# Prompt attention in blocks of 256 queries, two heads abreast, with fp32r scores and V as the stationary operand

## The chip, the cores and the metric

The kernel runs on one NeuronCore of a Trainium2 chip. The metric is the device time of one launch in microseconds. The time of before is the median of three runs. A profile is one further execution, recorded by the hardware profiler; times in its rows are microseconds from the start of the recorded span. PE is TensorE (PEld its weight loads), DVE is VectorE, ACT is ScalarE, POOL is GpSimd, SP is SyncE, which here only issues DMAs.

## What is computed

A two-layer decoder trunk of width 1024 serves one prompt of 1024 tokens and 8 sample requests of 4 new tokens each. Layer 0 mixes tokens with a causal convolution module, layer 1 with forgetting attention (16 heads of 64), and each is followed by a SwiGLU FFN. The change lies in the prompt part of layer 1's attention:

```python
c = jnp.cumsum(logf, axis=1)
s = jnp.einsum('bqhd,bkhd->bhqk', qi, k, preferred_element_type=jnp.float32) * scale
s = s + ci[:, :, :, None] - cT[:, :, None, :]
s = jnp.where(kpos[None, :] <= qpos[:, None], s, -jnp.inf)
pr = jax.nn.softmax(s, axis=-1)
return jnp.einsum('bhqk,bkhd->bqhd', pr.astype(v.dtype), v)
```

The term of the query's own c is the same for a whole row and falls out of the softmax; the kernel adds only the key's.

## The kernel before

All of the kernel is one launch with an instruction stream for each engine, ordered by semaphores. Most of its time goes to dense products: weights and activations are each split into a high and a low fp32r part, and three products hi*hi, lo*hi and hi*lo are summed in PSUM (`unit_block`, L673 to L675), over three blocks of 352 tokens. A "unit" is one 128-column slice of a weight, a pair of units is one step `q`. For each unit SP loads `wraw`, ACT writes `whi` (L1127), POOL writes `wlo` (L606), and PE waits for `w_lo`.

Three stages of layer 1 concern us, in this order.

1. Projection (24 units: 8 of q, 8 of k, 8 of v). DVE copies each unit from PSUM into `stg`, and ACT issues one DMA to a scratch tensor in HBM, `q_scr` or `k_scr` (`store_staged`), since attention needs heads on partitions 0 to 63. Keys and values are also transposed on PE for the outputs; the values stay in `Vt`, tokens on partitions. `negc`, the negative sum of the log forget gates, goes to `c_scr` through `negct`.

2. Prompt attention. It loops over 8 pairs of heads (`prompt_pair`), and in each over 16 tiles `t` of 128 queries: first the 8 of one head, then those of the other, in the order `ORDER = [3, 2, 1, 0, 7, 6, 5, 4]` of the query tile `qt`, each with its `(qt + 1) * 128` keys. For a tile PE makes the scores in fp32 from `qa` (64 rows of q and a row of ones) and `ka` (64 rows of k and the row of c) into two PSUM banks (L963); DVE adds the causal mask to the diagonal block (L1766) and takes the negative maximum (L1768); ACT takes exp with the sum as by-product (L1404) into `pr`, two buffers; PE transposes `pr` in blocks of 128 (L921), one tile late; ACT copies these to `pt` (L1391); PE multiplies, with `pt` as the stationary side and 64 columns of V moving (L937), two tiles late; DVE divides by the sum (L1745, L1751) into `on`; four such are transposed (L948) and copied to `OT` (L1756). SP loads a head's `qa` and `ka` when the tiles of the head before it have been scored (`load_head`). POOL has nothing to do.

3. Cache attention for the 8 requests. SP loads 64 pages of keys (`kr`) and 64 of values (`vr`), 512 KB each, four buffers of each; the first four key pages are issued while prompt attention still runs. PE transposes keys (L995), makes scores on four groups of 32 output partitions (L1011), and multiplies with the values likewise (L1050). The `cb_scr` scratch carries the sums of the cached gates (`cbT`), stored by ACT at the start of stage 2 (L1382).

The order of work within each engine is the order of the program; there are no priorities.

Of the kernel before, what the change touches and what calls it, by code (L numbers as in the profile page):

```python
# [28 lines left out]
F32 = mybir.dt.float32  # L29
# [7 lines left out]
P = 128  # L37
# [3 lines left out]
def hybrid_step(nc, x_prompt, x_sample, state_conv, cache_k, cache_v, cache_logf, page_table,  # L41
# [37 lines left out]
    with ExitStack() as ctx:  # L79
# [93 lines left out]
        negct = at("negct", [H, SEQ], F32, after("negc"))  # L173
        NM = at("NM", [NS, NREQ, H, TNEW], F32, after("negct"))
# [13 lines left out]
        qa = at("qa", [DH + 1, 2, SEQ], F32, where["xhi"][0])  # L188
        ka = at("ka", [DH + 1, 2, SEQ], F32, after("qa"))
        pr = at("pr", [P, 2, SEQ], F32, after("ka"))  # L190
        pt = at("pt", [P, 2, SEQ], F32, after("pr"))
        on = at("on", [P, NT, P], F32, where["tm"][0])
# [16 lines left out]
        ob = at("ob", [P, 2, P], F32, where["negct"][0])  # L209
# [4 lines left out]
        q_scr = nc.dram_tensor("q_scr", (D, SEQ), F32).ap()  # L214
        k_scr = nc.dram_tensor("k_scr", (D, SEQ), F32).ap()
        c_scr = nc.dram_tensor("c_scr", (H, SEQ), F32).ap()
# [58 lines left out]
        nqk = sem("nqk")  # L275
        stg_st = [sem("stg_st0"), sem("stg_st1")]
# [14 lines left out]
        a_ld = [sem("a_ld0"), sem("a_ld1")]  # L291
        a_sc = sem("a_sc")
        a_mk = sem("a_mk")
        a_max = sem("a_max")
        a_exp = sem("a_exp")
        a_tr = sem("a_tr")
        a_pt = sem("a_pt")
        a_pv = sem("a_pv")
        a_rec = sem("a_rec")
        a_on = sem("a_on")  # L300
        o_tr = sem("o_tr")
# [65 lines left out]
        NTILES = C * NTAU  # L367

        ORDER = [3, 2, 1, 0, 7, 6, 5, 4]
# [23 lines left out]
        def _(sp):  # L393
# [87 lines left out]
            load_pairs(Q_ATTN_OUT, 1, attn_w_out[0], 0, C, two)  # L481

            for s in range(2):
                sp.wait_ge(mm[s], Q_ATTN_OUT * NB)
            for s in range(2):
                sp.wait_ge(stg_st[s], 16 * C)
            sp.wait_ge(c_st, 16)

            def load_head(i, s):
                h = i * 2 + s  # L490
                sp.dma_start(qa[0:DH, s, :], q_scr[ds(h * DH, DH), :]).then_inc(a_ld[s], 16)
                sp.dma_start(ka[0:DH, s, :], k_scr[ds(h * DH, DH), :]).then_inc(a_ld[s], 16)
                sp.dma_start(ka[DH:DH + 1, s, :], c_scr[ds(h, 1), :]).then_inc(a_ld[s], 16)
            load_head(0, 0)
            load_head(0, 1)
            with sp.Fori(1, C) as i:
                for s in range(2):

                    sp.wait_ge(a_sc, i * NTAU + (NT * (s + 1) - NTAU))
                    load_head(i, s)  # L500
# [27 lines left out]
            for s in range(2):  # L528
                sp.wait_ge(kt_st[s], 16 * C // 2)
            for n in range(4):  # L530
                load_k(n)

            sp.wait_ge(a_pv, NTILES)
            sp.wait_ge(w_lo, 2 * Q_ATTN_OUT + 2)
# [7 lines left out]
            for n in range(NP):  # L542
                load_v(n)
                if n + NPG + 4 < NP:
                    load_k(n + NPG + 4)
                if n % NPG == 1 and n // NPG + 1 < NREQ:
                    load_sums(n // NPG + 1)
# [18 lines left out]
        def _(pool):  # L566
# [71 lines left out]
            with pool.Fori(Q_ATTN_IN + 1, QK) as q:  # L638
                low_parts(q)


            with pool.Fori(QK, Q_ATTN_OUT + 1) as q:
                low_parts(q)
# [3 lines left out]
            pool.wait_ge(a_pv, NTILES)  # L647
            nc.gpsimd.memset(cbx[:, :, :], 0.0).then_inc(d_z, 1)
            nc.gpsimd.memset(PTs[:, :, :, :], 0.0).then_inc(d_z, 1)
            nc.gpsimd.memset(PTn[:, :, :], 0.0).then_inc(d_z, 1)  # L650
            with pool.Fori(Q_ATTN_OUT + 1, Q_FFN1 + 1) as q:
                low_parts(q)
# [6 lines left out]
        def _(pe):  # L659
# [221 lines left out]
            pe.wait_ge(c_nc, 2)  # L881
# [32 lines left out]
            pe.wait_ge(a_ones, 1)  # L914

            def probs_tr(base, t):

                pe.wait_ge(a_exp, base + (t + 1))
                past(pe, a_pt, base + t)
                for kb in range(ORDER[t % NT] + 1):  # L920
                    m = nc.tensor.transpose(PS[:, 4 + kb // 4, (kb % 4) * P:(kb % 4 + 1) * P],  # L921
                                            pr[:, t % 2, kb * P:(kb + 1) * P], ident[:, :])
                m.then_inc(a_tr, 1)

            def values(i, base, t):

                pe.wait_ge(a_pt, base + (t + 1))
                past(pe, a_on, base + (t - 1))

                if t == NTAU - 1:  # L930
                    pe.wait_ge(o_ev, i * 2 + 1)
                elif t == 1:
                    past(pe, o_ev, i * 2)
                nb = ORDER[t % NT] + 1
                for kb in range(nb):
                    v = Vt[:, kb, ds(i * P + (t // NT) * DH, DH)]
                    m = nc.tensor.matmul(PS[:, 6 + t % 2, 0:DH],  # L937
                                         pt[:, t % 2, kb * P:(kb + 1) * P], v,
                                         start=(kb == 0), stop=(kb == nb - 1))
                m.then_inc(a_pv, 1)  # L940

            def outputs_tr(i, half):

                pe.wait_ge(a_on, i * NTAU + (NTAU - 2 + 2 * half))
                if half == 1:
                    pe.wait_ge(o_ev, i * 2 + 1)
                for j in range(4):
                    m = nc.tensor.transpose(PS[:, 7, j * P:(j + 1) * P], on[:, 4 * half + j, :], ident[:, :])  # L948
                m.then_inc(o_tr, 1)

            def prompt_pair(i):
                base = i * NTAU
                first = isinstance(i, int)
                for t in range(NTAU):
                    s, qt = t // NT, ORDER[t % NT]
                    if t % NT == 0:
                        pe.wait_ge(a_ld[s], i * 48 + 48)

                    past(pe, a_exp, base + (t - 1))
                    nk = (qt + 1) * P  # L960
                    for k0 in range(0, nk, 512):
                        k1 = min(nk, k0 + 512)
                        m = nc.tensor.matmul(PS[:, 2 * (t % 2) + k0 // 512, 0:k1 - k0],  # L963
                                             qa[:, s, qt * P:(qt + 1) * P], ka[:, s, k0:k1],
                                             start=True, stop=True)
                    m.then_inc(a_sc, 1)
                    if t >= 1:
                        probs_tr(base, t - 1)
                    elif not first:
                        probs_tr(base - NTAU, NTAU - 1)  # L970
                    if t >= 2:
                        values(i, base, t - 2)
                    elif not first:
                        values(i - 1, base - NTAU, NTAU + t - 2)
                    if not first and t in (0, 2):
                        outputs_tr(i - 1, t // 2)

            prompt_pair(0)
            with pe.Fori(1, C) as i:
                prompt_pair(i)  # L980
            probs_tr((C - 1) * NTAU, NTAU - 1)
            values(C - 1, (C - 1) * NTAU, NTAU - 2)
            outputs_tr(C - 1, 0)
# [937 lines left out]
```

## Time and profile before

| | us |
|---|---|
| median of 3 runs (lowest, highest) | 3260.32 (3250.59, 3261.3) |
| the profiled execution, its time | 3277.89 |
| its span | 3276.1 |
| mean granted clock of TensorE in it | 0.934 |
| projection of layer 1, from 1331 to 1637 | 306 |
| prompt attention, from 1652 to 2075 | 423 |
| cache attention, from 2077 to 2340 | 263 |

The span goes from the first to the last instruction; the execution's own time has 1.8 us around it. The granted clock is 1.00 at 2.4 GHz and 0.50 at 1.2 GHz.

### The profile page before, as it was taken

How to read it: one execution, taken by the hardware profiler on the slowest of the kernel's cores; microseconds unless marked ns; L12 is line 12 of the kernel's file. 1: busy time of each engine (PE TensorE's matmuls, PEld its weight loads, DVE VectorE, ACT ScalarE, POOL GpSimd, SP SyncE). 2: the span in 40 equal slices, each digit the busy share in tenths (PEclk: the TensorE clock that was granted, in tenths of full speed). 3: DMA queues.
4: the chain of work that ended last, by engine and by line, in shares of the span. 5: the costliest groups of instructions: out<-in, count | busy, mean ns of one | idle time of the engine just before them, and what ended most of it. 6: DMA issues, size and time to landing. Idle time of an engine off the chain costs nothing.

```text
span 3276.1 us, 49541 instructions
## 1 busy us (share of the span) xinstructions
PE 2939.1 (90%) x18658; PEld 2725.1 (83%) x18658; DVE 1095.4 (33%) x1876; ACT 924.1 (28%) x1533; POOL 782.6 (24%) x378
## 2 busy tenths in 40 slices
PE   5786698999999999999999999777799999999997
PEld 4786497999999998899977777555688999999997
DVE  5899634111111114411135445433332111111114
ACT  4555533211111113211124334322223212111123
POOL 2899423222221213311200000000022222222221
PEclk8888799999999999999969779978899999999998
DMA  3101011111111111234102001477411111111111
GB/s 93 39 26 33 19 45 33 40 50 45 36 49 37 53 40 50 73 86 113 42 24 74 20 19 45 167 253 275 151 39 39 37 53 39 44 45 37 53 35 69
DMA packets 243435, 206.63 MB, mean 63 GB/s; under 512 B 18188, under 2 KB 218892, under 8 KB 243076
## 3 DMA queue, kind: packets, MB, share of 16 engines
q1 hardware_dynamic: 230215, 186.66, 18.5%
q10 hardware_dynamic: 13133, 18.80, 1.7%
q8 instruction: 55, 0.90, 0.1%
q14 instruction: 32, 0.26, 0.0%
HBM read 183.16 MB, written 23.13 MB: 63 GB/s over the span
## 4 chain that ended last, share of the span: by engine, by line
PE 51%; issue 32%; POOL 8%; DVE 6%; ACT 2%; DMA 1%; DVEq 0%; ACTq 0%; SPq 0%; POOLq 0%
PE PS L673 17%; PE PS L675 16%; PE PS L674 16%; POOL yp L629 7%; DVE tm L1511 2%; POOL wlo L606 1%; DVE rs L1490 1%; DMA xin<-in_x_prompt 1%; DVE hlo L1553 1%; PE PS L800 0%; DVE xlo L1496 0%; ACT prods L1240 0%; ACT tm L1282 0%; ACT xhi L1138 0%; DVE yn L1884 0%
## 5 line engine op out<-in xcount | busy, mean ns | idle before, releaser
L673 PE MATMUL PS<-xhi,whi 128*128 128x352 f32 x3456 | 1144.8, 331 | 134.0 <-DVE u L1605 54.2
L675 PE MATMUL PS<-xlo,whi 128*128 128x352 f32 x3456 | 1121.7, 325 | 0.0
L674 PE MATMUL PS<-xhi,wlo 128*128 128x352 f32 x3456 | 1121.4, 324 | 0.0
L606 POOL TENSOR_TENSOR wlo<-wraw,whi 128x1024 fp32r<-128x1024 f32 x208 | 497.9, 2395 | 1867.0 <-ACT whi L1127 1867.0
L673 PEld LDWEIGHTS PS<-xhi,whi 128*128 128x128 f32 x3456 | 657.9, 190 | 177.8 <-DVE u L1605 56.1
L674 PEld LDWEIGHTS PS<-xhi,wlo 128*128 128x128 f32 x3456 | 661.0, 191 | 0.0
L675 PEld LDWEIGHTS PS<-xlo,whi 128*128 128x128 f32 x3456 | 658.9, 191 | 0.0
L1127 ACT ACTIVATE whi<-wraw 128x1024 fp32r<-128x1024 f32 x208 | 218.9, 1052 | 593.1 <-PE PS L675 565.1
L1548 DVE TENSOR_TENSOR ht<-PS,ht 128x352 f32<-128x352 f32 x132 | 69.1, 524 | 906.7 <-PE PS L675 902.7
L673 PE MATMUL PS<-hhi,whi 128*128 128x352 f32 x1056 | 341.2, 323 | 8.8 <-issue 8.8
L674 PE MATMUL PS<-hhi,wlo 128*128 128x352 f32 x1056 | 338.5, 321 | 0.0
L675 PE MATMUL PS<-hlo,whi 128*128 128x352 f32 x1056 | 338.2, 320 | 0.0
L1534 DVE TENSOR_TENSOR X<-PS,X 128x352 f32 x216 | 113.2, 525 | 447.3 <-PE PS L675 447.0
L673 PEld LDWEIGHTS PS<-hhi,whi 128*128 128x128 f32 x1056 | 198.1, 188 | 10.8 <-issue 10.8
L674 PEld LDWEIGHTS PS<-hhi,wlo 128*128 128x128 f32 x1056 | 198.4, 188 | 0.0
L675 PEld LDWEIGHTS PS<-hlo,whi 128*128 128x128 f32 x1056 | 197.9, 187 | 0.0
L629 POOL TENSOR_TENSOR yp<-yp,prods 128x1024 f32<-128x1024 f32 x80 | 191.1, 2388 | 11.8 <-POOL yp L629 0.4
L1628 DVE SCALAR_TENSOR_TENSOR PS<-u,par,PS 128x1024 f32<-128x1024 f32 x144 | 185.7, 1289 | 4.8
L963 PE MATMUL PS<-ka,qa 65*128 65x512 f32 (+3 forms) x384 | 182.8, 592 | 3.1 <-issue 3.1
L1182 ACT ACTIVATE hhi<-ht 128x352 f32 x132 | 65.5, 498 | 410.4 <-DVE ht L1548 410.4
L937 PEld LDWEIGHTS PS<-Vt,pt 128*128 128x128 f32 x1152 | 164.1, 221 | 11.9 <-issue 7.0
L937 PE MATMUL PS<-Vt,pt 128*128 (+1 forms) x1152 | 167.9, 299 | 3.6 <-DVE OT L1756 3.6
(184 smaller groups left out, 2386.9 us busy)
## 6 DMA issues: line engine op xcount, KB each, us to landing
wraw<-in_ffn_w_gu SPq DMA_DIRECT2D x88, 512.0 KB, 3.7
kr<-in_cache_k SPq DMA_DIRECT2D x64, 512.0 KB, 6.5
vr<-in_cache_v SPq DMA_DIRECT2D x64, 512.0 KB, 8.1
wraw<-in_ffn_w_down SPq DMA_DIRECT2D x32, 384.0 KB, 3.0
wraw<-in_attn_w_in SPq DMA_DIRECT2D x24, 512.0 KB, 3.8
wraw<-in_ffn_w_down SPq DMA_DIRECT2D x32, 320.0 KB, 2.8
wraw<-in_conv_w_in SPq DMA_DIRECT2D x16, 512.0 KB, 3.9
wraw<-in_conv_w_out SPq DMA_DIRECT2D x8, 512.0 KB, 3.5
```

The costliest lines, as they stand in the source:

```text
L606: nc.gpsimd.tensor_tensor(wlo[:, s, :], wraw[:, s, :], whi[:, s, :].bitcast(F32), ALU.subtract).then_inc(w_lo, 1)
L629: nc.gpsimd.tensor_tensor(yp[:, :], prods[:, 0, :] if i == 1 else yp[:, :], prods[:, i % 3, :], ALU.add).then_inc(p_tap, 1)
L673: nc.tensor.matmul(out, wh, hi[:, k, blk(b)], start=(k == 0), stop=False)
L674: nc.tensor.matmul(out, wl, hi[:, k, blk(b)], start=False, stop=False)
L675: m = nc.tensor.matmul(out, wh, lo[:, k, blk(b)], start=False, stop=(k == kc - 1))
L937: m = nc.tensor.matmul(PS[:, 6 + t % 2, 0:DH], pt[:, t % 2, kb * P:(kb + 1) * P], v, start=(kb == 0), stop=(kb == nb - 1))
L963: m = nc.tensor.matmul(PS[:, 2 * (t % 2) + k0 // 512, 0:k1 - k0], qa[:, s, qt * P:(qt + 1) * P], ka[:, s, k0:k1], start=True, stop=True)
L1127: nc.scalar.activation(whi[:, s, :], wraw[:, s, :], ACT.Copy).then_inc(w_hi, 1)
L1511: return nc.vector.scalar_tensor_tensor(tm[:, tmi(b, c), :], X[:, c, blk(b)], par[:, c, row:row + 1], rs[:, b, :], ALU.mult, ALU.mult)
L1534: nc.vector.tensor_tensor(xs, PS[:, NB * s + b, 0:BW], xs, ALU.add).then_inc(ev[s], 1)
L1548: nc.vector.tensor_tensor(ht[:, b, :], PS[:, NB + b, 0:BW], ht[:, b, :], ALU.mult).then_inc(ev[1], 1)
L1628: nc.vector.scalar_tensor_tensor(yacc, u[:, k:k + SEQ], w[:, R_DW + k:R_DW + k + 1], yacc, ALU.mult, ALU.add).then_inc(cv, 1)
```

## The change

Prompt attention is written anew, fully unrolled, and its inputs are prepared otherwise.

- Tiles: pairs of heads as before, but the tiles alternate between the heads, `qt` from 7 down to 0. Two query tiles of both heads make a block of 256 queries, 4 blocks in a pair, 32 in all.
- Scores: fp32r. While staging, ACT makes `sth`, the high part, POOL makes `stl`, the low part, and ACT issues three stores for each unit of q and two for each of k. `qa` is [hi; hi] on 128 rows, `kau` and `kal` are [lo; hi], `qb` is [lo; 1; 1] and `kbu`, `kbl` are [hi; c high; c low] on 66. The mask is added by PE, as a product of `identr` and `cmaskr`.
- The lower 512 keys are double buffered, the upper ones are loaded in two parts as they come free.
- P is divided by its sum before the transposes, on POOL, in place, with four buffers of `pr`. The transposes come three tiles late.
- Of the transposes' two PSUM banks ACT copies one and DVE the other, into `pta` or `ptb`, where the two query tiles of a block lie side by side; below `qt` 4 each tile uses one bank.
- Values: V is the stationary side (64 columns), 256 columns of P transposed move, head 0 writes output partitions 0 to 63 and head 1 64 to 127, in three portions that come between scores and transposes. The result lies as `OT` needs it, and DVE copies it.
- Buffers: `pr` lies over `stg` and `kr`, `ptb` over `cbT`, `sth` and `stl` over `Vt`. So exp waits for the stores of `cbT` and of the keys, max for those of `cbT`, and all key pages are loaded after attention. The first pair of weights of the output projection is loaded and split during stage 3.

```diff
-        ORDER = [3, 2, 1, 0, 7, 6, 5, 4]
+        def tile(g):
+            i, t = g // NTAU, g % NTAU
+            return i, t % 2, NT - 1 - t // 2
+        def portions(n):
+            kts = list(range(2 * block_of(n)[1] + 2))
+            a, e = (len(kts) + 1) // 3, (2 * len(kts) + 1) // 3
+            return [kts[0:a], kts[a:e], kts[e:]]
...
# SP
+            load_upper(0, SEQ - QW)
+            load_keys(0)
+            load_upper(0, HALF)
+            load_lower(0)
+            load_keys(1)
+            for i in range(1, C):
+                sp.wait_ge(a_sc, NTAU * (i - 1) + 4)
+                load_upper(i, SEQ - QW)
+                sp.wait_ge(a_sc, NTAU * (i - 1) + 8)
+                load_upper(i, HALF)
+                sp.wait_ge(a_sc, NTAU * i)
+                load_lower(i)
+                if i + 1 < C:
+                    load_keys(i + 1)
...
# POOL
+            def staged_lows(q):
+                for s in range(2):
+                    pool.wait_ge(w_hi, q * 2 + (s + 3))
+                    nc.gpsimd.tensor_tensor(wlo[:, s, :], wraw[:, s, :], whi[:, s, :].bitcast(F32),
+                                            ALU.subtract).then_inc(w_lo, 1)
+                    pool.wait_ge(qk_hi, q * 2 + (s + 1 - 2 * Q_ATTN_IN))
+                    nc.gpsimd.tensor_tensor(stl[:, s, :], stg[:, s, 0:SEQ], sth[:, s, :].bitcast(F32),
+                                            ALU.subtract).then_inc(qk_lo, 1)
...
+            for g in range(TILES):
+                i, h, qt = tile(g)
+                pool.wait_ge(a_rec, g + 1)
+                probs = pr[:, g % 4, 0:(qt + 1) * P]
+                nc.gpsimd.tensor_scalar(probs, probs, rden[:, g % NTAU:g % NTAU + 1], None, ALU.mult).then_inc(a_nrm, 1)
...
# PE
+            def prompt_scores(g):
...
+                past(pe, a_exp, g - 1)
...
+                for k0 in range(0, nk, HALF):
+                    n = min(nk - k0, HALF)
+                    out = PS[:, 2 * (g % 2) + k0 // HALF, 0:n]
+                    k1, k2 = (kau[:, h, 0:n], kbu[:, h, 0:n]) if k0 else (kal[:, i % 2, h, 0:n], kbl[:, i % 2, h, 0:n])
+                    last = k0 + n == nk
+                    nc.tensor.matmul(out, q1, k1, start=True, stop=False)
+                    nc.tensor.matmul(out, q2, k2, start=False, stop=not last)
+                m = nc.tensor.matmul(PS[:, 2 * (g % 2) + qt // 4, (qt % 4) * P:(qt % 4 + 1) * P], identr[:, :],
+                                     cmaskr[:, :], start=False, stop=True)
+                m.then_inc(a_sc, 1)
...
+            def prompt_values(n, part):
...
+                for kt in portions(n)[part]:
+                    c0 = P if kt == 2 * bn + 1 else 0
+                    for h in range(2):
+                        m = nc.tensor.matmul(PS[DH * h:DH * h + DH, 6 + n % 2, c0:QW],
+                                             Vt[:, kt, (2 * i + h) * DH:(2 * i + h + 1) * DH],
+                                             block_probs(n)[:, h, kt, c0:QW], start=(kt == 0),
+                                             stop=(kt == 2 * bn + 1), skip_group_check=True)
...
+            for g in range(TILES + 6):
+                if g < TILES:
+                    prompt_scores(g)
+                if g >= 7:
+                    n, part = divmod(g - 7, 4)
+                    if part < 3:
+                        prompt_values(n, part)
+                if 3 <= g < TILES + 3:
+                    probs_tr(g - 3)
...
# ACT
+            act.wait_ge(cb_st, 16 * NREQ)
...
+            for g in range(TILES + 3):
+                if g >= 3 and uses(g - 3)[0]:
+                    probs_out(g - 3)
+                if g < TILES:
+                    prompt_exp(g)
...
# DVE
+            dve.wait_ge(cb_st, 16 * NREQ)
+            for g in range(TILES + 6):
+                if g < TILES:
+                    prompt_max(g)
+                if 1 <= g <= TILES:
+                    prompt_rec(g - 1)
+                if 3 <= g < TILES + 3 and uses(g - 3)[1]:
+                    probs_out(g - 3)
+                if g >= 10 and (g - 10) % 4 == 0:
+                    outputs_out((g - 10) // 4)
```

## Rows read from the trace of the kernel before

**Rows 1.** the page: busy time of each engine, granted clock in 40 slices.

```profile
PE 2939.1 (90%) x18658; PEld 2725.1 (83%) x18658; DVE 1095.4 (33%) x1876; ACT 924.1 (28%) x1533; POOL 782.6 (24%) x378
...
PEclk8888799999999999999969779978899999999998
```

**Rows 2.** windows by stage: span, busy us (instructions), clock, DMA share, GB/s.

```profile
1331.00:1637.00 306.00, 295.43 (x1855) 290.65 (x1854) 51.24 (x116) 47.73 (x67) 59.88 (x27) 0.98 0.30 83
1652.00:2075.00 423.00, 400.53 (x2176) 309.83 (x2175) 199.67 (x528) 181.23 (x385) 1.87 (x2) 0.83 0.11 34
2077.00:2340.00 263.00, 191.33 (x2208) 139.62 (x2208) 88.58 (x113) 60.79 (x106) 0.00 (x0) 0.82 0.74 258
```

**Rows 3.** windows over one pair of heads, at full and at half clock.

```profile
1797.00:1842.00 45.00, 41.72 (x274) 32.44 (x274) 24.98 (x67) 22.58 (x49) 0.00 (x0) 1.00 0.10 23
1842.00:1920.00 78.00, 77.14 (x274) 60.56 (x273) 25.42 (x68) 22.39 (x49) 0.00 (x0) 0.52 0.05 14
```

**Rows 4.** waits within the pair at full clock: total us, times, longest.

```profile
ACT pt L1391 <- PE PS L921: 21.2, 17, 1.8
```

**Rows 5.** timeline of PE's loads within the pair: start, us, what, idle before.

```profile
1801.61 0.19 PEld L963 LDWEIGHTS PS<-ka,qa 65*128 65x128 f32 x1 [0.24 <-issue]
...
1802.79 0.75 PEld L921 LDWEIGHTS PS<-ident,pr 128*128 128x128 f32 x7 [0.99 <-ACT pr L1404]
...
1803.51 1.86 PEld L937 LDWEIGHTS PS<-Vt,pt 128*128 128x128 f32 x16
```

**Rows 6.** groups by form within the pair: busy us, mean ns, idle before.

```profile
L1766 DVE TENSOR_TENSOR PS<-PS,cmask 128x128 f32<-128x128 f32 x17 | 5.1, 298 | 8.2 <-PE PS L963 8.0
...
L1404 ACT ACTIVATION_READ_ACCUMULATOR pr<-PS,nmx 128x1 f32 x16 | 3.2, 198 | 0.0
L1745 DVE RECIPROCAL rden<-den 128x1 f32<-128x1 f32 x16 | 2.6, 163 | 11.8 <-PE PS L937 11.8
...
L1768 DVE TENSOR_REDUCE nmx<-PS 128x1 f32<-128x1024 f32 x2 | 2.4, 1224 | 0.1
L1404 ACT ACTIVATE pr<-PS,nmx 128x1024 f32<-128x1024 f32 x2 | 2.2, 1114 | 2.4 <-DVE nmx L1768 2.4
...
L1756 DVE COPY OT<-PS 128x512 f32 x2 | 1.4, 692 | 0.1
...
L1391 ACT ACTIVATE pt<-PS 128x512 f32<-128x512 f32 x2 | 1.2, 597 | 2.4 <-PE PS L921 2.4
...
L1404 ACT ACTIVATE pr<-PS,nmx 128x128 f32<-128x128 f32 x2 | 0.7, 367 | 0.5 <-DVE nmx L1768 0.5
L1768 DVE TENSOR_REDUCE nmx<-PS 128x1 f32<-128x128 f32 x2 | 0.6, 291 | 0.1
```

**Rows 7.** timeline of fp32r products in the projection.

```profile
1625.25 0.32 PE L673 MATMUL PS<-xhi,whi 128*128 128x352 f32 x1
...
1625.72 0.33 PE L673 MATMUL PS<-xhi,whi 128*128 128x352 f32 x1
```

**Rows 8.** timeline of PE and its loads in the cache stage.

```profile
2211.32 0.38 PEld L1050 LDWEIGHTS PS<-vr,PTs 128*32 128x32 f32 x16 [0.17 <-issue]
...
2211.90 0.86 PEld L995 LDWEIGHTS PS<-ident,kr 128*128 128x128 f32 x8 [0.20 <-issue]
...
2212.92 1.92 PE L1011 MATMUL PS<-KT,qx 128*32 128x512 f32 x16
```

**Rows 9.** POOL's groups over the whole span.

```profile
L606 POOL TENSOR_TENSOR wlo<-wraw,whi 128x1024 fp32r<-128x1024 f32 x208 | 497.9, 2395 | 1867.0 <-ACT whi L1127 1867.0
...
L648 POOL MEMSET cbx<- 128x2048 f32 x1 | 1.8, 1805 | 435.3 <-PE PS L937 435.3
```

**Rows 10.** timeline around the start and the end of prompt attention.

```profile
1648.85 5.04 ACTq L1382 DMA_DIRECT2D cb_scr<-cbT  x8
...
2087.73 3.05 PEld L995 LDWEIGHTS PS<-ident,kr 128*128 128x128 f32 x16 [4.97 <-DMA kr<-in_cache_k]
```

More of the change, by code:

```diff
@@ L496, in _, with rows, load_upper @@
[L496 to L500, printed above, removed]
+                sp.wait_ge(stg_st[s], 40 * C)
+            sp.wait_ge(c_st, 32)
+            def rows(scr, i, r0, r1, cols):
+                return scr[2 * i:2 * i + 2, r0:r1, cols].rearrange("h p t -> p h t")
+            def load_upper(i, c0):
+                cols, keys = slice(c0, c0 + QW), slice(c0 - HALF, c0 - HALF + QW)
+                sp.dma_start(qa[:, :, cols].bitcast(F32), rows(q_scr, i, 0, P, cols)).then_inc(a_up, 16)
+                sp.dma_start(kau[:, :, keys].bitcast(F32), rows(k_scr, i, 0, P, cols)).then_inc(a_up, 16)
+                sp.dma_start(qb[0:DH, :, cols].bitcast(F32), rows(q_scr, i, P, P + DH, cols)).then_inc(a_up, 16)
+                sp.dma_start(kbu[:, :, keys].bitcast(F32), rows(k_scr, i, DH, P + 2, cols)).then_inc(a_up, 16)
@@ L545, in _ @@
                     load_k(n + NPG + 4)
+                if n == 3 * NPG:
+                    load_pairs(Q_ATTN_OUT, 1, attn_w_out[0], 0, C, two)
                 if n % NPG == 1 and n // NPG + 1 < NREQ:
@@ L913, in _ @@
             pe.wait_ge(x_ev, 3)
[L914 to L976, printed above, removed]
@@ new lines, in probs_tr @@
+            def probs_tr(g):
+                i, h, qt = tile(g)
+                pe.wait_ge(a_nrm, g + 1)
+                if uses(g)[0]:
+                    past(pe, a_pta, NA[g])
+                if uses(g)[1]:
+                    past(pe, a_ptd, ND[g])
+                for kb in range(qt + 1):
+                    bank = 4 + kb // 4 if qt >= 4 else 4 + g % 2
+                    m = nc.tensor.transpose(PS[:, bank, (kb % 4) * P:(kb % 4 + 1) * P],
+                                            pr[:, g % 4, kb * P:(kb + 1) * P], ident[:, :])
+                    if kb in (3, qt):
+                        m.then_inc(a_tra if bank == 4 else a_trd, 1)
@@ new lines, in prompt_exp @@
+            def prompt_exp(g):
+                i, h, qt = tile(g)
+                nk = (qt + 1) * P
+                act.wait_ge(a_max, g + 1)
+                if g >= 4:
+                    if uses(g - 4)[1]:
+                        act.wait_ge(a_trd, ND[g - 4] + 1)
+                    else:
+                        act.wait_ge(a_tra, NA[g - 4] + 1)
+                t = g % NTAU
+                nc.scalar.activation(pr[:, g % 4, 0:nk], banks(2 * (g % 2), nk), ACT.Exp,
+                                     bias=nmx[:, t:t + 1], accum_out=den[:, t:t + 1]).then_inc(a_exp, 1)
@@ L1776, in _, with prompt_max @@
-            prompt_pair(0)
-            with dve.Fori(1, C) as i:
-                prompt_pair(i)
-            output(C - 1, (C - 1) * NTAU, NTAU - 2, False)
-            outputs_out(C - 1, 0)
-            output(C - 1, (C - 1) * NTAU, NTAU - 1, False)
-            outputs_out(C - 1, 1)
+            def prompt_max(g):
+                i, h, qt = tile(g)
+                t = g % NTAU
+                dve.wait_ge(a_sc, g + 1)
+                nc.vector.tensor_reduce(nmx[:, t:t + 1], banks(2 * (g % 2), (qt + 1) * P), AX.X, ALU.max,
+                                        negate=True).then_inc(a_max, 1)
```

281 lines of the change are left out of this document (163 added, 118 removed).

## The prediction

> **What bounds the kernel now.** I read the page first, for the engines' shares and the granted clock [rows 1], then a table of windows by stage [rows 2], then one pair of heads at each of TensorE's two clocks [rows 3], the waits inside the pair [rows 4], and the durations inside it [rows 5, 6]. PE is busy 90% of the span. The change lies in three of its stages: the q, k, v projection of layer 1 (306 us), prompt attention (423 us) and the attention over the cache (263 us) [rows 2]. In the first, PE is busy 295 of 306 us, POOL 60, ACT 48: others' new work has room there. In prompt attention PE is busy 400 us, DVE 200, ACT 181, POOL 2. The third is loosely bound: PE 191 of 263 us, with the DMA engines at 74%.
>
> The reader is to see in [rows 3] that a pair of heads (16 query tiles) takes 45 us at full clock and 78 at half, with DVE and ACT at 25 and 22 us either way: PE sets the pace at both. In [rows 4] ACT waits for PE's transposes 21 us of the 45.
>
> PE's 45 us can be rebuilt. A 65x512 fp32 score product is two instructions, each 0.19 us of load and 0.24 us of waiting for the stream, 0.43 us [rows 5]: 0.84 ns a column and instruction, 1.68 ns a column in all. A pair has 2 x 36 x 128 = 9,216 such columns: 15.5 us. Transposes are 7 in 0.75 us [rows 5], 0.107 each, 72 of them 7.7 us. Value products are 16 in 1.86 us [rows 5], 0.116 each, 144 of them 16.7 us: 64 columns stream while a 128-column load is what costs. Eight output transposes add 0.9. Sum 40.8; so 4.2 us of the 45 are lost between pieces. Eight pairs at 45 are 360 us; the other 63 of the 423 are the clock. It was 0.83 over the stage [rows 2], which is 34% of 423, or 144 us, at 1.2 GHz, and each us there loses 1 - 45/78 = 0.42 us: 61 us. The fall near 1842 comes in the middle of steady work that has not changed for two pairs, so the trace does not let me say when it will fall again.
>
> **Scores.** Each 512-key product becomes two fp32r ones (hi against lo and hi; lo and the ones row against hi and the c rows), and a 128-wide one adds the mask. The nearest row is the projection: three 352-wide fp32r instructions in 1625.72 - 1625.25 = 0.47 us [rows 7], 0.445 ns a column. 2 x 9,216 columns: 8.2 us. The mask product of 128 columns is likely bound by its 128-column load, as a transpose is: 0.107 x 16 = 1.7; if so short an fp32r stream runs at the fp32 rate it is 0.215 x 16 = 3.4. I take 1.7. Scores: 9.9 us instead of 15.5.
>
> **Transposes** stay, 7.7 us. The output transposes (0.9) go.
>
> **Values.** V (64 columns) is now loaded and 256 columns of P transposed stream past, in fp32. Two heads hold as many columns as the scores do, 9,216, at 1.68 ns: 15.5 us in a row, or 7.7 if head 0 and head 1 (output partitions 0 to 63 and 64 to 127) run at the same time. The cache stage shows the like: 16 fp32 instructions of 512 columns onto four groups of 32 output partitions took 1.92 us [rows 8], where one after the other they are 16 x 0.43 = 6.9. Four abreast ran nearly as four. I take 7.7, with 15.5 as the far end.
>
> The price is the change between narrow and full-width products, which comes twice in each of the 12 portions of a pair. In [rows 8] a group of 16 narrow instructions holds PE from 2211.32 to 2211.90, 0.58 us, for 16/4 x 128 columns at 0.84 ns = 0.43; the 8 transposes after it hold it from 2211.90 to 2212.92, 1.02 us, for 8 x 0.107 = 0.86. So a round trip costs 0.15 + 0.16 = 0.31 us, and 12 of them 3.8 us. The bounds are nothing and twice that. The gaps of 0.20 us before the transposes [rows 8] are this. The Trainium skill (TensorEngine Tiling (Array Packing), Key Properties) says that changing the tiling mode, not just the tile, drains TensorE; it gives no time, and speaks against cutting values into portions. The trace agrees, with the 0.31 us a round trip; without a drain the pair would be 3.8 us shorter.
>
> **PE's sum** for a pair at full clock is 9.9 + 7.7 + 7.7 + 3.8 = 29.1 us. Between pieces 4.2 us are lost now; the transposes may now lag three tiles and not one, but one more engine stands in the chain. From 0 to 4.2 I take 2.2: **31.3 us**. At half clock streams and loads double (15.4 + 3.4 + 15.3 + 15.4) and the changes cost perhaps 4 to 5: 54, with the loss **56 us**.
>
> **The other engines** for a pair. DVE keeps the max: the largest and smallest take 1.224 and 0.291 us with even steps between, 16 x 0.757 = 12.1 [rows 6]; reciprocals 2.6; it takes copies of the second PSUM bank, with 512 columns at 0.692 and 128 at about 0.29 [rows 6], 3.9 us for the upper tiles and 2.0 for one head's lower ones; outputs 4 x 0.42 = 1.7. It loses the mask adds (5.1) and the output scaling. Sum 22.3, with gaps about 24. ACT keeps exp, 16 x (1.114 + 0.367)/2 = 11.9, and the accumulator reads, 3.2, and copies 8 x 0.597 for the upper tiles and 1.75 for the lower: 21.6, with gaps 23 [rows 6]. POOL's scaling of P is not in the trace. One side is the two-input subtraction, 1024 columns in 2.395 us [rows 9]: at most 22 us a pair. The other is a fill, 2048 in 1.805, 0.88 ns a column [rows 9]: 8 us, with starts 10. I take near the latter, since one operand is read. The Trainium skill (GPSIMD Engine Reference, Engine selection) says that one-input work runs there at roughly line rate and two-input work at half the Vector engine's; no run here shows the former. By its rule or by either row PE is the longest: 29 against 24, 23 and 10 to 22. Only in the first four tiles of a pair (1024 and 896 wide) could POOL at the dear end, 9 us, pass PE, about 7.5; four buffers of P take up part. If that cover is gone it costs 1.5 us a pair, 12 in all.
>
> In order on each engine: a late scaling stalls PE at the transposes, and the next scores behind them. Before it, the copy after a transpose precedes exp on ACT, 0.6 + 1.3 us, while PE does one more round of some 2.5: it fits.
>
> **Edges of attention.** SP waits for the last projection product (near 1634), then issues ten loads, 2.3 MB, before the first scores. They should land near 1646, and PE comes to scores at 1651.7 now, so they are hidden. But exp and max must now wait until the cbT rows have been written: the eight stores are issued from 1648.85 for 5.04 us [rows 10], with landing near 1656; exp starts some 2 us later than now. Drain at the end about 6 us. Together 8.
>
> **Staging of q and k.** Twelve MB more are written, and per unit ACT gets one 1024-wide copy (about 1.05 us), POOL one subtraction (2.4 us), and SP nothing. A unit lasts about 306/24 = 12.7 us on PE. After a unit ends, ACT's copy, POOL's weight part, then its staged part, 6 us in all, precede ACT's next store, and ACT's next weight copy is due only when the other unit ends. Nothing is late: 0, at most 3 us. If it were late, PE's next unit would wait for its weight parts.
>
> **Cache stage.** The first four key pages can no longer be fetched during attention, since P lies over their buffers, and 1 MB of output weights moves into this stage: 4 us at 258 GB/s [rows 2]. The pages: PE now stands 4.97 us until 2087.73 for page 4 [rows 10], which also comes late, so the loss of the prefetch is partly hidden; 0 to 8 us. Two weight copies on ACT before the last request's are under the waits for V pages. All of it with staging: +5, from 0 to 15.
>
> **The sum.** With a quarter of the stage at half clock (now 34%), a pair takes 1/(0.75/31.3 + 0.25/56) = 35.2 us, eight 281, with the edges 289 us: 134 less than 423. With +5 elsewhere the profiled execution would go from 3277.9 to 3149 us. The median of the runs, 3260.3, is 17.6 below that execution; if they had less of the half clock, they have less to lose of it too. I take 120 off the median: **3140 us**.
>
> **Rivals.**
> *Values in series* (8%). For it: two instructions of one head follow each other before the other head's. Against it: the same order in the cache stage overlaps. A pair is then 39 and 71 us, in the mix 44: 8 x 44 + 8 = 360, a gain of 58: 3202.
> *The half clock lasts* (15%). Each pair ends in small tiles where PE may stand for max, exp and scaling, and where PE stands more the clock is lower (0.82 in the cache stage, with PE busy 73% [rows 2]); once there, it stayed 60 to 80 us in this stage. At 60% of the stage the pair is 42.6 us, 349 us in all: 3191.
> *POOL bounds* (5%): 1.5 us a pair more, or a little beyond: 3155 to 3170.
> *Slower* (4%): the clock stays at half through nearly the whole stage. Eight pairs at 56 and 8 are 456 us, +33, with +5 elsewhere: about 3298. It decides from a share of 88%, where a pair takes 51.3 us and the gain is used up. Against it: PE's stream is denser than now, with full-height products in place of 65 rows.
> *Nearly always full clock and cheap changes* (8%): 8 x 28 + 8 = 232: about 3078.
> The forecast itself keeps 60%, from 3105 to 3180.
>
> **Chances.** Runs agree within about 0.3%, so less than that can't be told from no change. Faster 0.94, within 0.3% 0.02, slower 0.04. The range reaches to the series case and the lasting half clock above and toward the cheap case below: 3085 to 3205.
>
> **What would show it.** A window over one pair at clock 1.00 should be 29 to 34 us, with the value products (128x256, 64 output partitions) in about 7.7 us and gaps near 0.2 us at both sides of each portion; POOL's multiply of 1024 columns between 0.9 and 2.4 us; DVE about 24 us of the pair. The page should show about 285 us of attention. I am wrong if PE waits for POOL at transposes, if value instructions of the two heads don't overlap, if the first scores come after 1656, if the projection stage grows beyond 310 us, or if the cache stage grows by more than 15.

## The result, and the profile after

The kernel became slower: 3400.78 us (median of four runs, 3399.67 to 3402.95) against 3255.45 us for the kernel before in the same session (3225.69 to 3261.3). The ratio is 1.047, with an interval of 1.040 to 1.053. Medians here are of all runs, while ratios and their 95% intervals leave out runs in a slower state (over 1.5% above the fastest of their kernel), so a ratio need not be the quotient of the two medians beside it. The forecast of 3140 us and its range both missed, and so did the sign.

The page of the changed kernel: the engines' busy time, two rows of the 40 slices, and two of its DMA issues (KB each, us from issue to landing, where the profile has it).

```profile
span 3401.1 us, 47969 instructions
...
PE 2811.3 (83%) x18210; PEld 2615.6 (77%) x18210; DVE 1058.2 (31%) x1736; ACT 907.0 (27%) x1517; POOL 1038.5 (31%) x522
...
PE   5777699999999998335739788866798999999997
...
PEclk8888799999999999767859899988799999999998
...
wraw<-in_attn_w_in SPq DMA_DIRECT2D x24, 512.0 KB, 15.1
...
q_scr<-sth ACTq DMA_DIRECT2D x16, 512.0 KB
```

PE has less work than before, 2811 us in place of 2939 [rows 1], and yet the span is 125 us longer. A hole stands in PE's row from the seventeenth to the twenty-first slice, 1360 to 1786 us. It is not in attention, as the windows of the same three stages show (to be laid beside [rows 2]):

```profile
1331.00:1895.00 564.00, 331.42 (x2062) 321.53 (x2062) 52.47 (x120) 63.15 (x83) 92.81 (x41) 0.78 0.22 71
1898.00:2187.00 289.00, 249.39 (x1728) 182.80 (x1728) 163.07 (x384) 148.41 (x353) 219.76 (x130) 0.96 0.30 92
2189.00:2466.00 277.00, 191.42 (x2208) 137.78 (x2208) 88.39 (x112) 62.34 (x108) 5.88 (x4) 0.83 0.74 255
```

Attention takes 289 us, to the microsecond what was forecast. The projection stage before it has grown so far that the first scores come at 1897.8 instead of 1651.7: +246 us. Attention gives 134 back, the cache stage takes 14 more, and what follows it is 1 us shorter. 246 - 134 + 14 - 1 = 125, which is the difference of the two profiled executions (3402.95 and 3277.89).

So the question is what PE waits for in the projection. The waits from 1331 to 1770, total us, times, longest:

```profile
POOL wlo L708 <- ACT whi L1205: 307.8, 16, 51.3
ACT whi L1205 <- issue: 273.0, 13, 35.7
...
PE PS L757 <- POOL wlo L708: 76.0, 6, 23.9
...
PE PS L900 <- DVE wfs L1796: 73.6, 1, 73.6
...
PE PS L919 <- ACT ktok L1414: 49.3, 6, 21.1
```

PE waits for weight parts of POOL, POOL for the weight copies of ACT, and ACT for "issue", that is for nothing on another engine. ACT's timeline says what it does in those gaps (start, us, what, idle before):

```profile
1376.53 1.04 ACT L1377 ACTIVATE sth<-stg 128x1024 fp32r<-128x1024 f32 x1
1377.80 25.57 ACTq L1383 DMA_DIRECT2D q_scr<-sth  x2
1403.58 9.59 ACTq L1386 DMA_DIRECT2D q_scr<-stl  x1
1413.27 1.06 ACT L1205 ACTIVATE whi<-wraw 128x1024 fp32r<-128x1024 f32 x1 [35.70 <-issue]
```

ACT issues three stores, and these three issues hold it 35.7 us. The next weight copy `whi` comes only behind them. In the trace of before the issue of a staged store took 0.34 to 0.55 us:

```profile
1353.89 0.34 ACTq L1298 DMA_DIRECT2D q_scr<-stg  x1
```

The DMA view of the changed kernel of 1375 to 1560 says why an issue takes so long:

```profile
DMA  1411111114111111411111141111111111111111
GB/s 53 151 52 52 52 53 52 52 53 152 52 51 53 52 53 52 151 52 52 52 53 53 52 151 52 51 53 53 51 53 53 53 51 53 53 53 51 53 53 53
...
q10 hardware_dynamic: 2336, 9.43, 12.4%
...
wraw<-in_attn_w_in SPq DMA_DIRECT2D x4, 512.0 KB, 15.3
```

Queue 10 carries ACT's stores. Its packets take 12.4% of 16 engines, without a pause: that is 2.0 engines, all the time. They move 9.43 MB in 185 us, 51 GB/s, so one store of 512 KB takes 10.3 us. The single packets in the trace say the same without an average. Those of the stores are 4,096 bytes and take 159 ns each, and for 92% of that window exactly two of them are under way at once; a store is 128 packets, two at a time 64 x 0.159 = 10.2 us. In the kernel before packets of the same size take 160 ns, but sixteen are under way at once. A store's destination is `scr[heads, r:r + DH, :]`, two heads by 64 rows by 1024, and two is the size of its outermost dimension. ACT can issue only as fast as the two engines drain. The 40 stores need 40 x 10.3 = 412 us; from the first at 1339 that reaches to 1751. The k units end at 1770, later by what the key outputs `ktok` take in the same queue and by some 20 us in which it stood empty. Before, the k units ended at 1530. That is 240 of the 246 us.

The Trainium skill (DMA: Bandwidth & Descriptors, Why a DMA increments its semaphore by 16 and not by 1) states this: the number of DMA engines is the largest up to 16 that divides the sizes of both sides' slowest dimension that isn't 1. Here that is 2, and the trace agrees, with 12.4% of 16 and two packets at a time.

### The profile page after: what moved, and what is told of

It reads as the page before. It is cut to its first block, busy times and chain, and to the rows that moved or that the text cites. A ratio compares the mean times of both kernels' runs of the same rounds, so it can differ in the third digit from the quotient of the medians.

```text
span 3401.1 us, 47969 instructions
## 1 busy us (share of the span) xinstructions
PE 2811.3 (83%) x18210; PEld 2615.6 (77%) x18210; DVE 1058.2 (31%) x1736; ACT 907.0 (27%) x1517; POOL 1038.5 (31%) x522
## 4 chain that ended last, share of the span: by engine, by line
PE 59%; issue 11%; POOL 10%; DVE 6%; DMA 4%; ACTq 4%; ACT 3%; SPq 1%; DVEq 0%; POOLq 0%
PE PS L757 17%; PE PS L759 17%; PE PS L758 17%; POOL yp L694 6%; POOL pr L726 2%; PE PS L1046 2%; DMA vr<-in_cache_v 2%; DVE tm L1619 2%; ACTq L1383 2%; DMA kr<-in_cache_k 2%; PE PS L1032 2%; PE PS L1073 1%; ACTq L1419 1%; DVE rs L1598 1%; ACTq L1386 1%
## 5 line engine op out<-in xcount | busy, mean ns | idle before, releaser
L671 POOL TENSOR_TENSOR wlo<-wraw,whi 128x1024 fp32r<-128x1024 f32 x192 | 459.5, 2395 | 1725.2 <-ACT whi L1205 1725.2
L726 POOL TENSOR_SCALAR pr<-pr,rden 128x896 f32<-128x896 f32 (+7 forms) x128 | 218.9, 1723 | 106.5 <-DVE rden L1866 105.6
L1254 ACT ACTIVATE ht<-PS 128x352 f32<-128x352 f32 x132 | 60.8, 464 | 368.0 <-PE PS L759 367.9
L1318 ACT ACTIVATE prods<-u,par 128x1024 f32<-128x1024 f32 x96 | 107.9, 1148 | 122.0 <-POOL yp L694 83.1
```

The costliest lines, as they stand in the source:

```text
L671: nc.gpsimd.tensor_tensor(wlo[:, s, :], wraw[:, s, :], whi[:, s, :].bitcast(F32), ALU.subtract).then_inc(w_lo, 1)
L726: nc.gpsimd.tensor_scalar(probs, probs, rden[:, g % NTAU:g % NTAU + 1], None, ALU.mult).then_inc(a_nrm, 1)
L1318: nc.scalar.activation(prods[:, i % 3, :], u[:, k:k + SEQ], ACT.Copy, scale=par[:, q, R_DW + k:R_DW + k + 1]).then_inc(a_tap, 1)
```

## The experiments

The theory (A): the shape of the stores confines each to two DMA engines. The rival (B): it is the volume of the stores, 20 MB, or the added work in ACT's and POOL's order. For attention the open points were the price of POOL's scaling, the cost of cutting the values into portions, and the late start.

**One head in each store.** The changed kernel, each store cut in two of 64 rows; bytes and order stay.

```diff
-                    act.dma_start(scr[heads, r:r + DH, :], sth[:, s, :].bitcast(F32)).then_inc(stg_st[s], 16)
+                    for h in range(2):
+                        act.dma_start(scr[head[h], r:r + DH, :].rearrange("a p t -> (a p) t"),
+                                      sth[DH * h:DH * h + DH, s, :].bitcast(F32)).then_inc(stg_st[s], 16)
```

> The changed kernel with one edit: each staged store of 128 rows (two heads, outer dimension 2 in HBM) becomes two stores of 64 rows, one per head, with 64 as the outer dimension on both sides. Bytes are the same. Theory A (the two-head pattern runs on two DMA engines: 64 packets of 159 ns, 10.2 us a store, 40 stores, 408 us in a row): the projection stage falls from about 550 us to 306 to 315, the kernel to about 3150 us. Theory B (the volume of the stores, or ACT's and POOL's extra work in order, is what holds the stage): the stage stays above 500 us and the kernel above 3370.

Measured: 3166.82 us (3166.78 to 3168.0), 234 less than the changed kernel; against before (3254.37, thirteen runs) the ratio is 0.971, interval 0.964 to 0.979. Its windows by stage, and DMA issues in the projection stage:

```profile
1331.00:1664.00 333.00, 308.63 (x2068) 303.11 (x2067) 55.48 (x123) 63.71 (x84) 93.67 (x42) 0.96 0.43 122
1665.00:1951.00 286.00, 246.73 (x1722) 180.94 (x1722) 162.52 (x383) 148.41 (x353) 219.15 (x129) 0.97 0.30 93
1954.00:2230.00 276.00, 190.46 (x2208) 136.87 (x2208) 88.38 (x112) 61.89 (x107) 6.30 (x4) 0.84 0.75 256
```

```profile
wraw<-in_attn_w_in SPq DMA_DIRECT2D x20, 512.0 KB, 4.9
q_scr<-sth ACTq DMA_DIRECT2D x32, 256.0 KB, 3.8
q_scr<-stl ACTq DMA_DIRECT2D x16, 256.0 KB, 4.9
```

Twice as many issues for the same bytes, and the stretch from 1331 to the first scores is back at 333 us from 567 (before: 321). The weights land in 4.9 us and not in 15. Theory A holds, B falls as the main cause: volume and added work are the same as in the changed kernel. A asked for 306 to 315 us of stage and about 3150, so some 17 us are left over; the first scores come at 1664.5, still 12.8 us later than before. That two engines are at work the packets show; that the size of two is what picks their number was not tried with any other size.

Where the 12.8 us lie can be read off PE's waits up to the first scores, in this kernel and then in the kernel before:

```profile
PE PS L900 <- DVE wfs L1800: 8.0, 1, 8.0
PE PS L940 <- ACT ktok L1418: 5.9, 1, 5.9
```

```profile
PE PS L816 <- DVE wfs L1688: 3.7, 1, 3.7
PE PS L856 <- ACT ktok L1324: 1.5, 1, 1.5
```

Both are at the end of a kind of units, the first after q, the second after k. There PE can't go on to another unit without them, and ACT comes to `wfs` and to the last `ktok` only behind the last unit's stores, whose issues and low part keep it 5.3 and 4.0 us. Together (8.0 - 3.7) + (5.9 - 1.5) = 8.7 us. After each stand PE's granted clock is lower than before's: 0.80 against 0.93 from 1412 to 1437, 0.77 against 0.96 from 1530 to 1560. What is lost there by the clock can make up the rest; it was not counted out.

**The kernel before, with that pattern.** Its 16 stores, same bytes, written with two heads outermost.

```diff
-                act.dma_start(scr[ds(q * (2 * P) + (s * P - q0 * 2 * P), P), :], stg[:, s, 0:SEQ]
+                act.dma_start(scr[ds(q * 4 + (2 * s - 4 * q0), 2), 0:DH, :], stg[:, s, 0:SEQ]
```

> The kernel before with one edit: its 16 staged stores use the two-head pattern (scratch rows of the changed kernel's shape, gaps between heads), bytes as before. Theory A: each such store takes about 10 us where it took 2.6 to 4.7 from issue to landing; with one a unit of 12.7 us most of it is hidden, so the kernel is 0 to 20 us slower. Theory B: landing stays at 2.6 to 5 us and the time is that of before.

Measured: 3280.06 us (ten runs, 3254.97 to 3302.51) against 3254.37 for the kernel before (thirteen, 3222.17 to 3289.04), ratio 1.011, interval 1.005 to 1.016. Both scatter by more than they differ (the means of all runs are 3279.8 and 3256.3), and A had asked for 20 us at most, so the total alone says little. The profile says more: the first scores come at 1663.7, 12 us late, and the weights and the key outputs land late, where the kernel before has 4.2 and 3.3 us:

```profile
wraw<-in_attn_w_in SPq DMA_DIRECT2D x20, 512.0 KB, 10.3
...
out<-ktok ACTq DMA_DIRECT2D x8, 512.0 KB, 9.2
```

Between 1331 and 1437 both kernels send the same 1,024 packets of 4,096 bytes from ACT's queue, at 160 ns and at 162 ns each: before mostly sixteen at once, some 13 us in all, here two at a time, over 89 us. PE loses its time at the same two places as in the first experiment: it waits 8.1 us for `wfs` after the last q unit and 5.5 for the last `ktok` (3.7 and 1.5 before). So the pattern alone confines the stores, and it does harm even where 16 of them have time to drain (16 x 10.3 = 165 us in a stage of 306). With 40 stores, 412 us, the slack is used up, and the price is 246 us. The two profiled executions differ by 19 us (3297.13 and 3277.89). Besides the 12, some 10 came up in attention, which ran at half clock in two periods of 82 us each and not of 61 and 82; no run ties that to the stores.

**Fewer stores of the slow kind.** The changed kernel with its two-head stores, but the high part of q written once and read twice by SP: 32 stores in place of 40.

```diff
-            (k_scr, (DH,), 0) if keys else (q_scr, (0, DH), P)
+            (k_scr, (DH,), 0) if keys else (q_scr, (0,), P)
```

> The changed kernel with its two-head stores, but the high part of q is stored once, not twice, and loaded twice (two loads of 64 rows). 32 stores instead of 40. Theory A (two DMA engines, 10.2 us a store, one after the other): the projection stage falls by 8 x 10.2 = 82 us, the kernel to about 3320 us. If the stage is held by something else than the number of such stores (ACT or POOL in order), it moves by less than 20 us.

Measured in one run: 3319.03 us, 82 less than 3400.78; eight stores are 8 x 10.2 = 82. In the profile the first scores come 79 us earlier (1819.0 and 1897.8). So each of these eight stores cost what the queue takes for one.

**POOL's part.** The kernel of the first experiment, but POOL scales only the first 128 columns of each tile. It leaves the division of the other columns out, so it serves for its time alone.

```diff
-                probs = pr[:, g % 4, 0:(qt + 1) * P]
+                probs = pr[:, g % 4, 0:P]
```

> As the first run, and POOL scales only the first 128 columns of each tile of P (the rest stays undivided): 16 x 0.60 = 9.6 us of POOL a pair instead of 27.4. If POOL is what sets the pair of 34.2 us, a pair falls to 29 to 31 us, where PE's own sum lies, and attention by 25 to 40 us. If it is PE or the coupling of scores, max and exp, a pair stays within 1 us of 34.2.

Measured in one run: 3144.65 us, 22 less than 3166.82. First POOL in the changed kernel: its group for 1024 and 128 columns, and a timeline over a pair.

```profile
L726 POOL TENSOR_SCALAR pr<-pr,rden 128x1024 f32<-128x1024 f32 x16 | 45.3, 2843 | 65.7 <-DVE rden L1866 65.7
...
L726 POOL TENSOR_SCALAR pr<-pr,rden 128x128 f32<-128x128 f32 x16 | 9.6, 602 | 17.9 <-DVE rden L1866 17.0
```

```profile
2016.49 20.28 POOL L726 TENSOR_SCALAR pr<-pr,rden 128x1024 f32<-128x1024 f32 x9 [1.78 <-DVE rden L1866]
...
2050.71 2.84 POOL L726 TENSOR_SCALAR pr<-pr,rden 128x1024 f32<-128x1024 f32 x1 [1.78 <-DVE rden L1866]
```

Nine tiles, of 1024 columns down to 512, follow each other without a gap; there POOL sets the pace, and PE's waits for it in that pair are:

```profile
PE PS L1032 <- POOL pr L726: 2.0, 3, 1.0
```

From pair to pair it is 2050.71 - 2016.49 = 34.2 us. With POOL's work cut the first maxima of two pairs stand 32.1 us apart, each waiting for PE:

```profile
1742.50 1.23 DVE L1864 TENSOR_REDUCE nmx<-PS 128x1 f32<-128x1024 f32 x1 [0.58 <-PE PS L1019]
...
1774.60 1.23 DVE L1864 TENSOR_REDUCE nmx<-PS 128x1 f32<-128x1024 f32 x1 [0.57 <-PE PS L1019]
```

So POOL costs 2.1 us a pair, 17 in the stage, and nearly all of the 32.1 is PE's own: PE stands for 1.8 of them. The pair did not come down to the 29 to 31 us expected, nor attention by 25 (from first scores to the cache stage it fell from 287 to 271). The other 5 of the 22 us lie outside attention and were not traced.

**The portions of the values.** The same kernel, again for its time alone, with all value products of a block in one portion instead of three, so that a pair changes 8 times less between narrow and full-width products, 4 in place of 12.

```diff
-            return [kts[0:a], kts[a:e], kts[e:]]
+            return [[], [], kts]
```

> As the run with POOL's work cut to 128 columns, and the value products of a block come in one portion, not three: 4 changes of width a pair and back instead of 12. By 0.31 us a round trip a pair should fall by up to 2.5 us against that run, if PE sets it. If a long portion makes PE late for max and exp, nothing or a loss.

Measured in one run: 3139.97 us; the pair goes from 32.1 to 31.3 us. That is 0.1 us for each round trip saved. The 0.31 of the forecast would have given 2.5. The same edit on the full kernel with the late waits of the next experiment:

> As the run with late waits (stores per head, POOL scales all of P), with a block's value products in one portion. With POOL's work cut short one portion gave 0.8 us a pair, not the 2.5 of my drain sum. If the drains cost what the gaps show, a pair of 34.2 us loses 0.8 or more here too and the kernel 5 to 10 us; if POOL holds the pair, under 3 us.

Measured: 3158.08 us (3154.54 to 3159.58) against 3158.15 without it, and the pair stays at 34.2. While POOL scales all of P, nothing is gained on PE.

**The start of attention.** In the changed kernel the first maximum stands long:

```profile
1907.95 2.36 DVE L1860 TENSOR_REDUCE nmx<-PS 128x1 f32<-128x1024 f32 x2 [10.23 <-DMA cb_scr<-cbT]
```

The first score product began at 1897.8, 10.1 us earlier. The issues of these stores had ended at 1899.6. ACT and DVE wait there for the stores of `cbT`, whose tile lies under one that attention writes. Here, on the kernel of the first experiment, both waits go to the seventh tile, ahead of the first write over `cbT`.

```diff
-            dve.wait_ge(cb_st, 16 * NREQ)
             for g in range(TILES + 6):
+                if g == 7:
+                    dve.wait_ge(cb_st, 16 * NREQ)
```

> The run with stores per head, and the waits of ACT and DVE for the stores of cbT moved from before the first tile to before the first copy into the buffer that lies over cbT (tile 4's copy). In the changed kernel the first maximum stood 10 us for those stores. If they were the last thing missing, the time falls by 8 to 11 us against the run with stores per head (3166.8); if the first tiles then wait for the loads of q and k, by less than 3.

Measured: 3158.15 us (3156.71 to 3160.22), 8.7 less than the first experiment. The first maximum now comes 2.3 us after the first score product begins (1663.81 and 1661.55), so 10.1 - 2.3 = 7.8 us of lateness are gone; the pair is unchanged at 34.2.

**Another engine for half of the scaling.** Two kernels, both built on the one with late waits: head 1's tiles are scaled by DVE, right after the reciprocal, or by ACT, after the next exp.

```diff
+                if h == 1:
+                    dve.wait_ge(a_rec, g + 1)
+                    probs = pr[:, g % 4, 0:(qt + 1) * P]
+                    nc.vector.tensor_scalar(probs, probs, rden[:, t:t + 1], None, ALU.mult).then_inc(a_nrd, 1)
```

> As the run with late waits, and head 1's tiles of P are scaled by DVE, head 0's by POOL as before. POOL's work in a pair halves, 27.4 to 13.7 us; DVE gets 4608 columns, 5 to 6 us a pair if it runs near one column a cycle. If POOL alone holds the pair above the 32.1 us seen with short scaling, a pair falls from 34.2 to about 32 us and the kernel by 15 to 18 us against the run with late waits. If DVE, now 24 to 25 us of a pair and in the chain between scores and exp, is then late, the pair stays at 33.5 or more.

Measured: 3153.6 us (3152.48 to 3159.07), ratio 0.969 (0.965 to 0.973). The pair takes 34.1 us although POOL is busy only 13.95 of them (window below). Together with the high part of q stored once:

> All of it: stores per head, high part of q stored once, late waits, head 1 scaled by DVE. The store per head is hidden already, so leaving 4 MB out should give 0 to 3 us on top of the run where DVE scales.

Measured: 3153.73 us, no different. Eight units' second store of q is worth nothing to leave out once the stores are quick.

Now ACT's version:

```diff
+            def prompt_scale(g):
+                act.wait_ge(a_rec, g + 1)
+                probs = pr[:, g % 4, 0:(qt + 1) * P]
+                nc.scalar.activation(probs, probs, ACT.Copy, scale=rden[:, g % NTAU:g % NTAU + 1]).then_inc(a_nra, 1)
```

> As the run with late waits, and head 1's tiles of P are scaled by ACT, after the exp of the next tile; DVE's chain is left as it is. ACT gets 4608 columns, 5 to 6 us a pair on top of 17. If DVE's own scaling is what ate the gain in the run where it scaled, a pair falls from 34.2 to 32 to 32.7 us and the kernel by 12 to 17 us; if any extra work on an engine between scores and transposes eats it, the pair stays at 33.5 or more.

Measured: 3139.84 us (3138.6 to 3139.99), ratio 0.964 (0.957 to 0.971). A window over one pair, for DVE's version and for ACT's:

```profile
1735.20:1769.30 34.10, 30.54 (x220) 22.47 (x216) 24.20 (x57) 18.43 (x44) 13.95 (x8) 1.00 0.33 94
```

```profile
1734.09:1766.29 32.20, 30.38 (x218) 22.30 (x220) 20.32 (x48) 23.60 (x54) 13.78 (x8) 1.00 0.34 101
```

The added work is of the same size, DVE 3.9 us and ACT 5.2, and neither engine is near its limit. What differs is the place in the order. PE stands 3.6 us of a pair with DVE scaling and 1.8 with ACT scaling, and 1.4 of these 1.8 us of difference lie just ahead of value products. Over two pairs PE's waits at the value products are, with DVE scaling and then with ACT scaling:

```profile
PE PS L1049 <- issue: 3.0, 5, 0.7
```

```profile
PE PS L1049 <- issue: 0.3, 2, 0.2
```

On DVE the scaling stands ahead of its copies of P transposed, for which the transposes' banks and the value products wait; PE's timeline of that kernel has such a wait, a short one:

```profile
1748.32 0.96 PE L1035 MATMUL PS<-ident,pr 128*128 128x128 f32 x7 [0.33 <-DVE pta L1887]
```

On ACT it stands behind the exp of the next tile, and ahead of a copy that comes one round later. That this order makes the 1.9 us between the two was argued from these waits, not tested by a third order.

**All together**: ACT's version, one portion, the high part of q stored once.

> As the run where ACT scales head 1, with the value products in one portion and the high part of q stored once. ACT's scaling brought 18 us, more than the 12 to 17 I gave it; the other two did nothing alone with POOL's full work. With POOL out of the way one portion may give its 0.8 us a pair, 6 us: about 3134. If not, 3139.

Measured: 3137.07 us (3134.03 to 3140.06), ratio 0.967 (0.960 to 0.974), the pair 32.4 us. That can't be told from ACT's version alone, so one portion did not give the 6 us hoped for. Value products take 1.1 us of PE less in a pair, but PE now stands some 1.1 us more ahead of the transposes. These two are the fastest, some 3.5% ahead of the kernel before.

## Why the prediction was wrong

**The step that failed** is the staging of q and k: "Nothing is late: 0, at most 3 us". It counted ACT's copy, POOL's part and the bytes, and priced each issue at nothing. The count of stores was right (three for a unit of q, two of k); that the new scratch shape puts two heads outermost, and so sends each store through two DMA engines at 10.2 us apiece, was not looked at. An issue then held ACT some 10 us and not nothing, and ACT's weight copies, POOL's weight parts and PE's next unit came late in turn. The price is 246 us, of which the first experiment gives 233 back by the shape alone. The other 12.8 us are the same term on a small scale: the longer order on ACT is hidden within a unit, but not after the last unit of q and of k, where PE waits 8.7 us more, with a lower clock behind each stand; the other 4 us were not counted out. The text named the sign of it ("if the projection stage grows beyond 310 us") but no rival priced it.

**Attention** came out at the forecast 289 us by luck, with terms that missed on both sides.

- Scores: a 512-wide fp32r product every 0.235 us, 0.459 ns a column; forecast 0.445. The rate was right, the term was not: counted from the start of each product to the start of the next, scores hold PE 12.9 us of a pair (in the 32.1 us pair with POOL's work cut), forecast 9.9. The mask products take 2.8 of that and not 1.7, and the rest is short products and the first one after transposes, which a rate by the column leaves out.
- Values: the two heads do run abreast. The timeline of the loads:

```profile
2028.88 1.08 PEld L1046 LDWEIGHTS PS<-pta,Vt 128*64 128x64 f32 x12
2030.34 0.64 PEld L1032 LDWEIGHTS PS<-ident,pr 128*128 128x128 f32 x6 [0.39 <-issue]
```

  12 products of 256 columns take 2030.34 - 2028.88 = 1.46 us. In series at 0.84 ns a column they are 2.58, abreast 1.29, plus one change between tilings of about 0.17. Right; that rival falls.
- Changes between tilings: the change stands in the trace, 0.17 on one side. But a round trip saved gave 0.1 us and not 0.31, so the term of 3.8 us a pair was too high. Values and changes together hold PE 9.5 us of that pair, forecast 7.7 + 3.8 = 11.5.
- PE's pair: 32.1 us with POOL out of the way, forecast 31.3: scores 3.0 over, values and changes 2.0 under, transposes 7.9 for 7.7, losses 1.8 for 2.2. Near, but by errors that cancel. The half-clock pair of 56 us has a slip too, scores doubled to 15.4 and not 16.4; it moves the forecast pair by 0.1 us.
- POOL: taken at 10 us a pair, with a dear end of 22. It is 27.4 us (2.5 ns a column and 0.28 us), outside both. The nearest row would have been the two-input subtraction [rows 9], not the fill, and even that is quicker, 2395 ns for 1024 columns against 2843. Within attention the rival "POOL bounds", 5%, is what happened: PE waits for POOL at the transposes, and it costs 2.1 us a pair against the 1.5 given. The Trainium skill (GPSIMD Engine Reference, Engine selection), by whose rule one-input work runs at about line rate, doesn't agree with this row: a multiply by a scalar of each partition runs slower than two-input work.
- The clock: forecast a quarter of the stage at 1.2 GHz. The stage's mean was 0.96, so 8% of it, about 23 us, was at half, all of it in the first 30 us. The rival that it lasts falls. This made up for POOL: eight pairs at 34.2 are 274 us; at the forecast mix they would have been 8/(0.75/34.2 + 0.25/56) = 303.
- Edges: 15 us (289 - 274) in place of 8. The first maximum was 7.8 us late and not 2: the `cbT` stores were taken to land 2 us after their last issue, and the maximum starts 8.4 us after it. The clock of the first tiles is in it too.

**Cache stage:** +14 us, forecast 5 with up to 15. Mis-sized but inside. With no key page fetched ahead PE waits 18.3 us for key pages in place of 9.3, and 34.2 for value pages in place of 25.8.

With the store shape mended the kernel takes 3166.8 us: 27 above the forecast and inside its range. Against the 3149 us forecast for the profiled execution it is 18: 13 in the projection stage, 8 in the cache stage beyond its +5, and 3 less in attention (286 for 289). The other 9 are the step from 3149 to 3140, which took the new kernel to share in the scatter of the old one; its four runs lie within 1.3 us of each other.

## What to carry to other kernels

Price a DMA by its access pattern and not by its bytes: look at the outermost size on both sides, and in the trace at what share of 16 engines a queue holds when it never pauses. A slow store is not off the path when a compute engine issues it: here, while earlier stores had not drained, each issue held ACT about 10 us, and everything behind it in ACT's order was late. Where work is moved to another engine, look at which copies and maxima stand behind it there: scaling on ACT gave 2.0 us a pair, nearly the same work on DVE 0.1.

## What the runs showed of the hardware that was not expected

- A DMA issue on ACT took 0.34 to 0.55 us while the queue drained and, with the two DMA engines of its stores saturated, mostly 3 to 17 us, some 10 a store; ACT did no other work in it. SP's loads suffered with it: `wraw` landed in 15 us (4.9 with the mended stores). A likely reason is that they share those two engines; the profile doesn't name the engines, and this was not tried.
- POOL's multiply by a scalar of each partition takes 2.5 ns a column in fp32; DVE does the 1024 columns in about 0.76 us and ACT in 1.14 us.
- The granted clock. The old attention ran at half in two periods, at its start and again in the middle of steady work [rows 3], 61 and 82 us long, and 82 and 82 in the second experiment's kernel. The eleven profiles with the new attention show half clock only in its first 30 us, and 0.96 to 0.98 as the stage's mean. Why the old one falls in mid-stage was not tried.
